# One add chain on Pool for the norm of a head group, direct sums in the first and last task, and later or smaller pieces elsewhere: a four-layer hybrid decoder step on eight cores

## The reference, cut to what matters

```python
a = rmsnorm(h, g_mix); z = a @ w_in
y_a = gate_b * dwconv3(gate_c * xa)                       # 384 channels
y_b = gelu(u) * (W_s[h] @ layernorm(gelu(v)) + b_s[h])    # 384 channels, within chunks of 128
y_c = silu(layernorm(dwconv31(glu(c_in)) + bias))         # 256 channels
mixed = concat(rmsnorm(y_a, g_a), rmsnorm(y_b, g_b), rmsnorm(y_c, g_c))
h = h + mixed @ w_out
f = rmsnorm(h, g_ffn); h = h + (silu(f @ w_gate) * (f @ w_up)) @ w_down
h = h + sigmoid(rmsnorm(h, g_ple) @ w_ple_gate) * (p[i] @ w_ple_proj)
```

## Time and profile before

| | |
|---|---|
| median of 3 runs | 3370.72 us (3369.08 to 3371.53) |
| the profiled execution: time / span of the slowest core (core 2) | 3370.0 / 3368.6 us |
| spans of the eight cores | 3354.7 to 3368.6 us |
| PE busy | 3238.8 us, 96% of the span |
| DVE / ACT / Pool busy | 57% / 49% / 23% |
| mean granted TensorE clock, cores | 0.985 to 0.988 |
| read from HBM, written | 673.71 MB, 12.78 MB |

### The profile page before, as it was taken

The page is one execution under the profiler, slowest core; times in us unless marked ns, Lnnn a source line. Parts: engine busy times, 40 slices in busy tenths (PEclk is TensorE's granted clock), DMA queues, the critical chain, the costliest instruction groups (busy, mean ns, idle before and its releaser), DMA issues.

```text
span 3368.6 us, 65137 instructions; the slowest of 8 cores (3354.7 to 3368.6 us)
## 1 busy us (share of the span) xinstructions
PE 3238.8 (96%) x22388; PEld 2026.6 (60%) x22388; DVE 1922.0 (57%) x3789; ACT 1645.5 (49%) x2518; POOL 789.3 (23%) x1172
## 2 busy tenths in 40 slices
PE   5889999999999999999999999999999999999997
PEld 2455556666665555665666565666666566566674
DVE  4824664583583575466466458357447546845835
ACT  5533555355366364355546635536445644553613
POOL 2020232232122123122213213222312311221312
PEclk9999999999999999999999999999999999999998
DMA  6476566766667557667666565765666755676684
GB/s 158 78 144 104 91 121 121 100 117 114 108 108 130 95 90 141 107 103 127 104 117 126 98 101 90 140 110 98 130 110 102 137 91 103 126 138 102 115 145 95
DMA packets 149327, 381.91 MB, mean 113 GB/s; under 512 B 20880, under 2 KB 73232, under 8 KB 149008
## 3 DMA queue, kind: packets, MB, share of 16 engines
q0 software_dynamic: 92864, 330.28, 58.6%
q1 hardware_dynamic: 56144, 47.47, 4.8%
HBM read 673.71 MB, written 12.78 MB: 204 GB/s over the span
## 4 chain that ended last, share of the span: by engine, by line
PE 89%; DMA 4%; DVE 3%; SPq 2%; issue 1%; ACT 1%; POOL 0%; DVEq 0%; ACTq 0%; POOLq 0%
PE PS L413 84%; DMA Y<-GB 2%; PE PS L622 2%; PE PS L497 1%; DVE NRM L514 1%; SPq L609 1%; SPq L401 1%; PE PS L482 1%; DMA MSLOT<-w_mix 1%; DMA FSLOT<-w_ffn 1%; DVE TMP L476 1%; PE PS L764 1%; DMA BSP<-bsP 0%; DVE TMP L936 0%; DMA H<-xin 0%
## 5 line engine op out<-in xcount | busy, mean ns | idle before, releaser
L413 PE MATMUL PS<-NRM,FSLOT 128*128 128x384 bf16 (+1 forms) x9984 | 1633.9, 318 | 10.4 <-DVE TMP L936 4.0
L413 PEld LDWEIGHTS PS<-NRM,FSLOT 128*128 128x128 bf16 x9984 | 975.9, 98 | 580.9 <-issue 32.3
L413 PE MATMUL PS<-NRM,MSLOT 128*128 128x384 bf16 (+1 forms) x4608 | 782.5, 319 | 12.1 <-DVE NRM L514 11.1
L413 PE MATMUL PS<-ACTB,FSLOT 128*128 128x384 bf16 (+1 forms) x4608 | 766.9, 317 | 1.2 <-DMA FSLOT<-w_ffn 0.5
L405 POOL DMA_DIRECT2D FSLOT<-w_ffn x468 | 254.1, 543 | 1590.7 <-PE PS L413 1466.5
L413 PEld LDWEIGHTS PS<-NRM,MSLOT 128*128 128x128 bf16 x4608 | 451.7, 98 | 279.9 <-issue 24.4
L891 DVE TENSOR_TENSOR ACTB<-TMP,PS 128x384 bf16<-128x384 f32 (+1 forms) x528 | 276.8, 530 | 589.3 <-PE PS L413 513.9
L413 PEld LDWEIGHTS PS<-ACTB,FSLOT 128*128 128x128 bf16 x4608 | 446.7, 98 | 262.5 <-issue 8.9
L889 ACT ACTIVATE TMP<-PS 128x384 f32<-128x384 f32 (+1 forms) x528 | 244.5, 472 | 595.7 <-PE PS L413 512.2
L910 DVE TENSOR_TENSOR H<-H,PS 128x384 f32<-128x384 f32 (+1 forms) x576 | 303.1, 530 | 300.8 <-PE PS L413 297.1
L472 ACT ACTIVATE TMP<-H 128x768 bf16<-128x768 f32 (+1 forms) x312 | 245.4, 804 | 229.0 <-DVE H L910 114.3
(11 more groups left out here) (86 smaller groups left out, 1924.7 us busy)
## 6 DMA issues: line engine op xcount, KB each, us to landing
FSLOT<-w_ffn POOLq DMA_DIRECT2D x420, 512.0 KB, 6.5
MSLOT<-w_mix POOLq DMA_DIRECT2D x84, 768.0 KB, 8.5
MSLOT<-w_mix POOLq DMA_DIRECT2D x36, 512.0 KB, 6.0
FSLOT<-w_ffn POOLq DMA_DIRECT2D x48, 384.0 KB, 4.6
Y<-GB SPq DMA_DIRECT2D x128, 103.0 KB, 10.9
y<-H SPq DMA_DIRECT2D x10, 768.0 KB, 10.8
H<-xin SPq DMA_DIRECT2D x6, 768.0 KB, 16.1
Y<-GB SPq DMA_DIRECT2D x32, 144.0 KB, 10.8
```

The source lines that it names most:

```text
L413: ops.append((lambda e, out_f=out_f, l_=l_, r_=r_, i=i, n=len(pairs): e.matmul(out_f(), l_(), r_(), start=(i == 0), stop=(i == n - 1)), li ...
```

## The change

Seven edits go together. (1) The sum for 3 chunks gets a path in which ACT squares two chunks and then one, Pool adds the first two in 32 bits and then the third (result in bf16), and PE sums that one chunk. It is used in tasks 1 to 11. (2) In task 0, and in the norms of kind `rf` of task 11 (ahead of the FFN, ahead of the PLE, the final one), the 8-chunk sums go without DVE's adds: PE takes all 8 squared chunks. (3) `CLS_IN` goes from 8 to 14 for the input norm of tasks 1 to 11, its `rstd` gets the same class, and its multiplies class 9 in place of 1; `MIX_TILES` goes from 186 to 182. (4) Half of the last task's PLE adds go from Pool to DVE. (5) In the final norm of the last block ACT multiplies 3 chunks by the gain and Pool by rstd, DVE does 5; `y` of the last third is written in pieces of 2 chunks in place of 4. (6) `CW` of layer 0 is loaded first of all. (7) `H` of thirds 1 and 2 is loaded after earlier events of task 0: after the first C gate and after the first convolution, and the plan takes the loads of third 0 as about twice as long.

```diff
-CLS_IN = 8.0
+CLS_IN = 14.0
+CLS_NRM = 9.0
-MIX_TILES = 186
+MIX_TILES = 182
...
-            if len(chunks) == 8 and T2:
+            if len(chunks) == 8 and paired:
...
+            if len(chunks) == 3 and paired:
+
+                bk, s0, s1, acc = Val("ps"), Val("tmp"), Val("tmp"), Val("tmp")
+                act(lambda e: e.activation(SQ[:, s0.i, :, 0:n], src(chunks[0], 2), AF.Square),
+                    2 * n, [keys(c) for c in chunks[0:2]], [s0], alloc=[s0, s1, acc], after=after, cls=cls)
+                act(lambda e: e.activation(SQ[:, s1.i, 0, 0:n], src(chunks[2], 1), AF.Square),
+                    n, [keys(chunks[2])], [s1], after=after, cls=cls)
+                pool(lambda e: e.tensor_tensor(TMP[:, acc.i, 0:n], SQ[:, s0.i, 0, 0:n], SQ[:, s0.i, 1, 0:n], ALU.add), n, [s0], [acc])
+                pool(lambda e: e.tensor_tensor(SQ[:, s1.i, 0, 0:n], TMP[:, acc.i, 0:n], SQ[:, s1.i, 0, 0:n], ALU.add), n, [acc], [s1])
+                P.add("pe", [(lambda e: e.matmul(bank(bk, n), ONES[:], SQ[:, s1.i, 0, 0:n], start=True, stop=True),
+                              [s1, ("ONES",)], [bk], [], None, 1)], n * COL, pos=cur[0].pos() - 0.02, alloc=[bk])
+                cur[0].w += n * COL
+                return bk
...
-            bk = sums(list(range(8)), n, src, keys, after, cls=cls)
-            rb = rstd(bk, n, 1.0 / D, kind)
+            bk = sums(list(range(8)), n, src, keys, after, cls=cls, paired=task > 0 and not (task == NTASK - 1 and kind == "rf"))
+            rb = rstd(bk, n, 1.0 / D, kind, cls)
             if final:
...
+                split = 5 if t == NT - 1 and b == 1 else 8
+                for c in range(split, 8):
+                    act(lambda e, c=c: e.activation(src(c, 1), src(c, 1), AF.Copy, scale=gain(c)), n, [("VEC",)], [keys(c)], cls=CLS_EV)
+                    pool(lambda e, c=c: e.tensor_tensor(src(c, 1), src(c, 1), rbt(rb, n), ALU.mult), n, [rb], [keys(c)])
+                scaled(rb, list(range(split)), n, src, keys, gain, lambda c: src(c, 1), keys, 0.0)
             else:
                 scaled(rb, list(range(8)), n, src, keys, lambda c: vcol(l, goff, c),
-                       lambda c: nrm(buf, c, b, n), lambda c: ("N", buf, c, b), 1.0)
+                       lambda c: nrm(buf, c, b, n), lambda c: ("N", buf, c, b), CLS_NRM if cls else 1.0)
...
-                bk = sums(chunks, n, src, keys)
+                bk = sums(chunks, n, src, keys, paired=task > 0)
...
-                    pool(lambda e, ti=ti, m=m: e.tensor_tensor(H[:, m, g0:g0 + n], TMP[:, ti.i, 0:n], H[:, m, g0:g0 + n], ALU.add),
-                         n, [ti], [("H", t, m, b)])
+                    (dve if task == NTASK - 1 and m % 2 else pool)(
+                        lambda e, ti=ti, m=m: e.tensor_tensor(H[:, m, g0:g0 + n], TMP[:, ti.i, 0:n], H[:, m, g0:g0 + n], ALU.add),
+                        n, [ti], [("H", t, m, b)])
...
+                    w = 2 if t == NT - 1 else 4
+                    for k0 in range(0, 8, w):
...
+        dma(CW[:], cw[0], 32000, writes=[("CW",)])
         dma(VEC[:], vec, 100000, writes=[("VEC",)])
...
-            if k < NT:
-                for b, (g0, n, _) in enumerate(THIRDS[k]):
-                    w = 4 if k else 2
+            for t in ((0,), (1, 2), ())[min(k, 2)]:
+                for b, (g0, n, _) in enumerate(THIRDS[t]):
+                    w = 4 if t else 2
                     for k0 in range(0, 8, w):
-                        dma(H[:, k0:k0 + w, g0:g0 + n], xin[:, k0:k0 + w, g0:g0 + n], 512 * w * n,
-                            writes=[("H", k, k0 + c, b) for c in range(w)], after=[("G", 0, 1)] if k else [])
+                        dma(H[:, k0:k0 + w, g0:g0 + n], xin[:, k0:k0 + w, g0:g0 + n], (512 if t else 1000) * w * n,
+                            writes=[("H", t, k0 + c, b) for c in range(w)], after=(None, [("G", 0, 0)], [("Y", 6, 0)])[t] if t else [])
```

More of the change, by code:

```diff
@@ L462, in proj, with sums @@
                                               [sk, ("N", buf, kc, b)]) for kc in range(ks)], [out_v])
-        def sums(chunks, n, src, keys, after=(), copy=False, cls=0.0):
-            if len(chunks) == 8 and T2:
+        def sums(chunks, n, src, keys, after=(), copy=False, cls=0.0, paired=True):
+            if len(chunks) == 8 and paired:
                 bk, sqs = Val("ps"), []
@@ L502, in sums, with rstd @@
             return bk
-        def rstd(bk, n, inv_n, kind):
+        def rstd(bk, n, inv_n, kind, cls=0.0):
             rb = Val(kind)
@@ L508, in rstd @@
                           (lambda e: e.activation(rbt(rb, n), rbt(rb, n), AF.Exp, scale=-0.5), [], [rb], [], None, 1)],
-                  0.55 + 0.0015 * n, pos=cur[0].pos(), tab="lnexp", alloc=[rb])
+                  0.55 + 0.0015 * n, pos=cur[0].pos(), tab="lnexp", alloc=[rb], cls=cls)
             return rb
@@ L527, in keys, with gain @@
                 return ("H", t, c, b)
-            bk = sums(list(range(8)), n, src, keys, after, cls=cls)
-            rb = rstd(bk, n, 1.0 / D, kind)
+            bk = sums(list(range(8)), n, src, keys, after, cls=cls, paired=task > 0 and not (task == NTASK - 1 and kind == "rf"))
+            rb = rstd(bk, n, 1.0 / D, kind, cls)
             if final:
-                scaled(rb, list(range(8)), n, src, keys, lambda c: VEC[:, DEPTH * NVL + c:DEPTH * NVL + c + 1],
-                       lambda c: src(c, 1), keys, 0.0)
+                def gain(c):
+                    return VEC[:, DEPTH * NVL + c:DEPTH * NVL + c + 1]
+                split = 5 if t == NT - 1 and b == 1 else 8
[3 more added lines that the diff above has]
+                scaled(rb, list(range(split)), n, src, keys, gain, lambda c: src(c, 1), keys, 0.0)
             else:
                 scaled(rb, list(range(8)), n, src, keys, lambda c: vcol(l, goff, c),
-                       lambda c: nrm(buf, c, b, n), lambda c: ("N", buf, c, b), 1.0)
+                       lambda c: nrm(buf, c, b, n), lambda c: ("N", buf, c, b), CLS_NRM if cls else 1.0)
         def mixer(task):
@@ L547, in mixer @@
             if t == 0:
-                dma(CW[:], cw[l], 32000, writes=[("CW",)])
+                if task:
+                    dma(CW[:], cw[l], 32000, writes=[("CW",)])
                 dma(LNB[:], lnb[l], 393000, writes=[("LNB",)])
@@ L948, in ffn @@
                     hnorm(task, b, 0, "rf", final=True)
-                    for k0 in range(0, 8, 4):
-                        dma(y_o[:, k0:k0 + 4, g0:g0 + n], H[:, k0:k0 + 4, g0:g0 + n], 2048 * n,
-                            reads=[("H", t, k0 + k, b) for k in range(4)])
+                    w = 2 if t == NT - 1 else 4
+                    for k0 in range(0, 8, w):
+                        dma(y_o[:, k0:k0 + w, g0:g0 + n], H[:, k0:k0 + w, g0:g0 + n], 512 * w * n,
+                            reads=[("H", t, k0 + k, b) for k in range(w)])
+        dma(CW[:], cw[0], 32000, writes=[("CW",)])
         dma(VEC[:], vec, 100000, writes=[("VEC",)])
```

## The result

The changed kernel takes 0.9899 of the time before, 95% interval 0.9875 to 0.9923: 3337 us by that ratio, against 3338 forecast. The profiled execution took 3334.36 us, with a span of 3332.8 on core 0, the slowest. Some executions ran with one or both dies at a lower granted clock; the ratio leaves them out.

A forecast was written before the change was run, and what follows sets the result against it. PE, busy 3238.8 of a 3368.6 us span, was taken as the bound. Terms of 6.3 + 5 + 2 + 11 + 8 = 32 us less than 3370.0 gave 3338 us, likeliest case 3330 to 3347, whole range 3318 to 3360.

The forecast's parts named there:

- PE's columns: Summing matmuls on PE: 13.5 us less in tasks 1 to 11, 3.9 and 3.3 us more for direct sums, net 6.3 less.
- Pool's adds cost nothing: Head groups' sums: 88 Pool adds, 97 us, covered by other PE work; 0 taken, bound +22 us.
- 802 ns for a DVE multiply beside Pool: DVE multiplies with two SBUF inputs while Pool adds: 802 ns each against 540 alone, at most some 32 us longer busy.
- the 4 us for the last multiplies: Last block's final norm: five DVE multiplies, 2.7 us alone or 4.0 beside Pool, three on Pool 3.3; 4 us taken.
- The start: Up to 109 us: 8.8 us gained less 4 of delay, 5 us less (bounds 9 less, 3 more).
- the first projection at 19.3: Task 0: logarithm first and direct sums let PE's first projection start at about 19.3 us, 5.8 us earlier.
- the 4 us allowed for copies and weights behind the moved loads: Between 30 and 80 us: 2.6 MB more of `H`, 11 us of transfer, taken as 4 us of delay.
- The hole at 109 to 123: PE busy 1.14 of 14 us; task 1's input norm multiplies go behind the head groups': 2 us less (0 to 6).
- The congestion: 160 to 206 us: third 2's `H` load leaves the shifted copies' queue, 11 us less of 12.4 (bounds 0 and 14).
- Elsewhere: Other waits ahead of norm sums, 18.7 us in 7: later classes may end or double them; 0 taken, 6 either way.
- The end: After the last PLE matmuls: earlier sums, split multiplies, smaller last write; end at 3360.5 against 3368.6, 8 us less (5 to 10).

The follow-up runs named there:

- The other start: Changed kernel with first weights loaded without waiting for `H`, and `H` of third 1 after the second C gate: median span 3316.8 us against 3323.6, ratio to before 0.9827.
- one other constant: Changed kernel with MIX_TILES 186 in place of 182, which adds or removes no work: median span 3339.7 us against 3323.6, 16.1 us more.

## Why the prediction was right, and which steps were not

**PE's columns: right.** 6.3 us net were forecast, with 9.0 after 300 us. Taking the Pool sums out adds 12.1 us of busy time after 300 us, and putting them alone into the kernel before takes 12.6 us of busy time off and 12.0 off the median span. In all PE's busy time fell by 8.6 us where 2.7 were counted. The mean granted clock rose from 0.987 to 0.990 and was left out of the forecast; that fewer stretches follow an idle PE is the likely reason, but it was not traced.

**Pool's adds cost nothing: right in the changed kernel.** Each takes 0.93 us of 384 columns (Pool is busy 70.8 us more and not 97: the 88 adds take 78 us, and half of the last PLE adds have left it), and two more per head group change nothing. Alone in the kernel before, they came with 5 us more of idle PE. The Trainium skill's advice against them ("GPSIMD Engine Reference", "Engine selection") calls GpSimd about twice as slow on two inputs. The trace agrees that it is slower, 1.5 times for this add (0.93 us, against 0.63 for DVE's add of the same shape and types), but PE bounds this kernel.

The forecast's 802 ns for a DVE multiply beside Pool against 540 ns alone compares two different things. 540 ns is what each of 8 multiplies adds to the run; the duration of each is 614 ns. And of the 16 of the earlier trace rows, 13 took 0.60 us and three took longer, 2.46, 1.35 and 1.18 us. What it costs DVE here is a few long stalls and not a slower pace. In the sum only the 4 us for the last multiplies hung on it.

**The start: wrong, 5 us forecast, nothing or less found.** Two steps failed: the first projection at 19.3, which came at 27.54, and the 4 us allowed for copies and weights behind the moved loads. In the changed kernel (core 0):

```profile
11.05 0.58 POOL L406 DMA_DIRECT2D MSLOT<-w_mix  x1 [2.44 <-DMA H<-xin]
...
16.22 0.58 ACT L520 ACTIVATE RB<-PS,EPSC 128x384 f32<-128x384 f32 x1 [1.04 <-PE PS L511]
...
25.98 0.80 PE L511 MATMUL PS<-TMP,ONES 128*128 128x384 bf16 x2 [3.56 <-ACT TMP L507]
26.95 0.80 PE L511 MATMUL PS<-TMP,ONES 128*128 128x384 bf16 x2 [0.17 <-ACT TMP L507]
...
27.54 6.15 PE L414 MATMUL PS<-NRM,MSLOT 128*128 128x384 bf16 x23
33.91 6.82 PE L414 MATMUL PS<-NRM,MSLOT 128*128 128x384 bf16 x41 [0.21 <-DVE CW L572]
48.94 2.75 PE L642 MATMUL PS<-Y,WD 128*32 128x384 bf16 x32 [8.22 <-DMA Y<-GB]
```

The same point in the kernel before (core 2):

```profile
40.14 4.22 PE L413 MATMUL PS<-NRM,MSLOT 128*128 128x384 bf16 x25 [0.21 <-DVE CW L552]
44.29 1.48 PE L622 MATMUL PS<-Y,WD 128*32 128x384 bf16 x32
```

The logarithm does come 6.8 us earlier than in the earlier trace rows, as forecast. But direct sums are PE's, and PE's queue is in order too: the 8 sums of block 1, each pair of them waiting for a piece of `H`, stand ahead of block 0's projection. I had looked at ACT's queue and not at PE's. The first loads of `H` also came late enough that the weights behind them were asked for at 11.05 in place of 8.29. Yet what the late first projection lost was made good: the 64 projection matmuls of the C units end at 40.7 us, against 44.3 before, close to the 3 us that the forecast had for that point. What was lost for good came after it: the convolution of block 0 waits 8.22 us, to 48.9, for copies whose transfer shares the DMA engines with third 1's load, so that it starts 4.6 us later than before and not 3.6 earlier. The other start shows what that was worth.

**The hole at 109 to 123: wrong in its place.** The multiplies of task 1's input norm still stand ahead of a head group's, and the output projection starts 3.6 us later than before:

```profile
121.37 4.84 DVE L528 SCALAR_TENSOR_TENSOR NRM<-H,VEC,RB 128x384 bf16<-128x384 f32 x9
...
126.89 3.46 PE L414 MATMUL PS<-NRM,MSLOT 128*128 128x384 bf16 x9 [5.26 <-DVE NRM L528]
```

In the kernel with the classes alone it starts at 120.23, 3 us earlier than before, near the forecast 2 us.

**The congestion: the size right, the cause only half.** 11 us were forecast; PE's idle time between 162 and 206 us fell by 10.4, and putting the load back costs 11.6, of which the wait is 7.6. SP's queue after shows the load of third 2 at 61.6 us, and the copies of task 1 at 158.6 as forecast. But a late copy costs only what PE has not got to do in its place: in the kernel before with the classes alone the load stays, and the wait is gone all the same. So in that kernel this term and the classes' term cover the same wait. It depends on the whole order: the changed kernel with the load put back has the classes too, and the wait stands there. The single effects of the change (9 to 12 for the Pool sums, 23 to 30 for the classes, 12 for the load, 5 for the end) sum to more than the 40 us by which the median span fell.

**Classes: the failed step is "Elsewhere".** I took 0 with 6 us either way for the middle, and 2 for the hole. Alone they are worth 29.6 us and within the change 22.6. The forecast read the waits row by row and asked which of them the classes touch, the input norm's sum. They changed most where they aren't seen: in the order that the planner gives PE around the convolutions, and with it how far PE is by 300 us. Why a later input norm makes the planner put FFN work there was not traced, and the three edits of the classes were not run one by one. That stays open. So does whether these classes are better or only lucky: one other constant moved the order by 16 us, though the effect here is larger and shows in both kernels.

**The end: right, 8 forecast, 6.8 found.** The changed kernel's last 14 us (core 0):

```profile
3317.95 0.56 DVE L959 TENSOR_TENSOR H<-TMP,H 128x384 f32<-128x384 f32 x1
3318.14 0.47 ACT L520 ACTIVATE RB<-PS,EPSC 128x256 f32<-128x256 f32 x1
...
3319.24 5.90 DVE L528 SCALAR_TENSOR_TENSOR H<-H,VEC,RB 128x256 f32<-128x256 f32 x13 [0.73 <-ACT RB L522]
...
3321.63 0.52 ACT L522 ACTIVATE RB<-RB 128x384 f32<-128x384 f32 x1
3322.30 5.60 POOL L550 TENSOR_TENSOR H<-H,RB 128x384 f32<-128x384 f32 x3 [5.42 <-ACT RB L522]
```

The multiplies could start 5.2 us after the last product, 1 us sooner than forecast. DVE does its 13 in 5.90 us and ends at 3325.1, but Pool's three take 5.60 in place of 3.3 and end at 3327.9, so that Pool and not DVE sets the last write. From there to the end of the span it is 4.9 us, where the forecast had 3 for the write. So 1 us sooner, then 1.6 more for the multiplies (4 were forecast) and 1.9 more for the write.

That the total came out within 2 us rests on errors that cancel: some 6 us too much for what lies ahead of 300 us (15.4 forecast: 5, 2 and 11 less the 3.9 of task 0's columns and with the 1.3 of task 1's; 9.7 found), and some 10 too little for the middle, where 0 was forecast beside the columns.

## What to carry to other kernels

When one engine is 96% busy and all queues are written ahead, ask of each late transfer what the busy engine could do meanwhile; where the wait stands in that queue is worth as much as the transfer. When work moves to another engine, read that engine's queue too: direct sums took adds from DVE and put PE behind loads that it had not waited for. A large change to a planned order should be tested edit by edit, in the old kernel and in the new one, since the effects overlap.

## What the runs showed of the hardware that was not expected

A Pool multiply of 128x384 beside DVE's multiplies with two SBUF inputs took 3.70 us, and 0.99 when DVE was done. The line's instructions, core 0:

```profile
L550 POOL TENSOR_TENSOR H<-H,RB x3: 988/988/3696, 3322.3 to 3326.9; 128x384 f32<-128x384 f32 x3
```

It is no chance: on all eight cores the first of the three took 3.69 to 3.70 us. DVE's own five of 384 columns took 0.61 us each there, as they do alone. DVE's run of 13 ended at 3325.1, and Pool's first multiply at 3326.0, 0.9 us later, which is less than it takes alone: it got next to nothing done before DVE was through. Between 430 and 456 us the delay showed on DVE: its multiply at 433.10, which took 2.46 us in place of 0.60, overlaps two Pool adds that began at 433.18 and took 1.95 together. In both places one engine stood for about as long as the other worked; which of them stands was not tested, and the spans of Pool are rough.
